# Expert token lists through a table in memory, a split distance that shrinks, and every second down weight left in f32, in a one-core hybrid decoder layer

## The reference

```python
g_sel = argmax(x @ w_rg + b_rg)                    # one of 4 groups per token
top_v, top_i = top_k(e_logits of that group, 2)    # two of its 4 experts
top_w = softmax(top_v) * softmax(g_logits)[g_sel]
gates = sum(one_hot(g_sel * 4 + top_i, 16) * top_w)
for e in range(16):
    h = silu(x @ w_g[e]) * (x @ w_u[e])            # 1024 -> 512
    out += gates[:, e] * (h @ w_d[e])              # 512 -> 1024
```

## Time and profile before

| | |
|---|---|
| median of 3 runs | 964.55 us (960.51 to 964.68) |
| the profiled execution | 964.39 us, span of its trace 962.6 us |
| mean granted clock of TensorE in it | 0.957 of full |
| busy over the span | PE 91%, DVE 68%, ACT 50%, POOL 8% |
| HBM read and written | 170.67 MB and 14.39 MB |

### The profile page before, as it was taken

The page is one execution under the profiler, slowest core; times in us unless marked ns, Lnnn a source line. Parts: engine busy times, 40 slices in busy tenths (PEclk is TensorE's granted clock), DMA queues, the critical chain, the costliest instruction groups (busy, mean ns, idle before and its releaser), DMA issues.

```text
span 962.6 us, 19161 instructions
## 1 busy us (share of the span) xinstructions
PE 876.3 (91%) x8176; PEld 585.2 (61%) x8176; DVE 658.8 (68%) x877; ACT 481.0 (50%) x681; POOL 81.8 (8%) x89
## 2 busy tenths in 40 slices
PE   6999999999999998999999979948899999888683
PEld 4444794856756655444444439947687777776561
DVE  5668769632887766643453344466799999998878
ACT  5434473323554445233223223554597878787842
POOL 8000000003000000000000000000121232111100
PEclk9999999999999999999999999967899999999987
DMA  8711414526731012953432416374899999999852
GB/s 213 168 35 45 125 30 110 155 66 176 188 91 34 25 37 61 372 137 98 121 102 83 122 28 220 127 284 140 305 359 383 399 397 397 381 392 378 331 203 90
DMA packets 122607, 178.20 MB, mean 185 GB/s; under 512 B 13357, under 2 KB 98661, under 8 KB 114326
## 3 DMA queue, kind: packets, MB, share of 16 engines
q1 hardware_dynamic: 116272, 162.76, 49.6%
q0 software_dynamic: 5968, 13.61, 5.2%
q10 hardware_dynamic: 278, 0.56, 0.2%
HBM read 170.67 MB, written 14.39 MB: 192 GB/s over the span
## 4 chain that ended last, share of the span: by engine, by line
PE 64%; DVE 19%; DMA 7%; ACT 6%; issue 3%; DVEq 0%; SPq 0%; ACTq 0%; POOLq 0%
PE bank L980 17%; PE bank L982 17%; PE bank L981 17%; DVE arena L1737 10%; DMA arena<-in_moe_wu 6%; ACT arena L853 3%; PE bank L1193 3%; PE bank L1212 3%; PE bank L1087 1%; PE bank L1202 1%; DVE arena L1844 1%; DMA arena<-x_rows,token_of 1%; DVE arena L1854 1%; ACT arena L935 1%; PE bank L1284 1%
## 5 line engine op out<-in xcount | busy, mean ns | idle before, releaser
L980 PE MATMUL bank<-arena 128*128 128x96 f16 (+3 forms) x2336 | 510.0, 264 | 37.4 <-DVE arena L1844 26.4
L981 PE MATMUL bank<-arena 128*128 128x96 f16 (+3 forms) x2336 | 509.0, 264 | 0.0
L982 PE MATMUL bank<-arena 128*128 128x96 f16 (+3 forms) x2336 | 508.6, 264 | 0.3
L980 PEld LDWEIGHTS bank<-arena 128*128 128x128 f16 (+1 forms) x2336 | 238.2, 102 | 139.4 <-issue 34.1
L982 PEld LDWEIGHTS bank<-arena 128*128 128x128 f16 (+1 forms) x2336 | 237.4, 102 | 77.1 <-issue 1.7
L981 PEld LDWEIGHTS bank<-arena 128*128 128x128 f16 (+1 forms) x2336 | 237.5, 102 | 68.2 <-issue 1.6
L1737 DVE SCALAR_TENSOR_TENSOR arena<-arena 128x2048 f16<-128x2048 f32 x96 | 216.9, 2287 | 49.2 <-ACT arena L853 46.8
L853 ACT ACTIVATE arena<-arena 128x2048 f16<-128x2048 f32 x96 | 180.6, 1904 | 12.5 <-DMA arena<-in_moe_wu 5.5
L620 ACT ACTIVATE arena<-arena 128x1024 f16<-128x1024 f32 (+1 forms) x92 | 92.5, 1007 | 101.3 <-PE bank L982 73.2
L1482 DVE SCALAR_TENSOR_TENSOR arena<-arena 128x1024 f16<-128x1024 f32 (+1 forms) x91 | 103.5, 1163 | 11.7 <-ACT arena L620 10.1
L674 ACT ACTIVATE arena<-bank 128x512 f32<-128x512 f32 x35 | 20.8, 595 | 90.4 <-PE bank L982 90.3
(11 more groups left out here) (275 smaller groups left out, 726.5 us busy)
## 6 DMA issues: line engine op xcount, KB each, us to landing
arena<-in_moe_wg SPq DMA_DIRECT2D x32, 1024.0 KB, 17.4
arena<-in_moe_wu SPq DMA_DIRECT2D x32, 1024.0 KB, 16.1
arena<-in_moe_wd SPq DMA_DIRECT2D x32, 1024.0 KB, 23.6
arena<-in_w_gate SPq DMA_DIRECT2D x32, 512.0 KB, 4.0
arena<-in_w_in SPq DMA_DIRECT2D x31, 512.0 KB, 4.2
arena<-in_w_branch SPq DMA_DIRECT2D x32, 192.0 KB, 3.5
y_rows<-in_c_tab SPq DMA_DIRECT2D x4, 1024.0 KB, 12.5
arena<-in_w_out SPq DMA_DIRECT2D x8, 512.0 KB, 5.3
```

The source lines that it names most:

```text
L980: pe.matmul(outb, lhs[0], rhs[0], start=first, stop=False, skip_group_check=True)
L981: pe.matmul(outb, lhs[0], rhs[1], start=False, stop=False, skip_group_check=True)
L982: return pe.matmul(outb, lhs[1], rhs[0], start=False, stop=last_, skip_group_check=True)
```

## The change

1. **Lists.** The 16-expert one-hots, `all_tokens`, `tell_lists` and `all_slots` go. VectorE computes for each token and choice j the place `rank * 16 + expert` in a table (`spots`, 6 small operations before the lists of the near experts are read). GpSimd stores 8 bytes per token there (token, token + 512 j) with 8 indirect stores of 128 entries, half of them after the gather of expert 0, half after that of expert 1. Then it loads the table (`lists`, 128 x 128 bytes) and stores the weights (1024 single values). Gathers from expert 2 on wait for the table. The weights of the last two experts are fetched by two indirect gathers. The near lists of experts 0 and 1 stay one-hot products. The table is filled with "nowhere" at the kernel's start.
2. **Buffers.** As the large one-hot is gone, chunk 16 takes the twelfth buffer and waits only for the x rows (it took buffer 5, after the split of chunk 5).
3. **Split distance.** ScalarE and VectorE split chunk c + 5 at step c up to step 55, c + 4 from 56 to 63, c + 3 from 64 to 71, and c + 2 from step 72 on.
4. **Down weights in f32.** For odd experts the d chunks aren't split. TensorE multiplies f32 hidden values (`hid_whole`) with the f32 chunk itself: 4 products of 512 columns for a half. Their buffer is free only when TensorE has used it, and SyncE waits for that.
5. **The end.** `add_rows` of the tiles 0 and 1 come at step 92, of tile 2 at step 93, of tile 3 at step 94 (one at each of the steps 92 to 95).

```diff
-LOOK = 5
+LOOK, LOOK_END = 5, 2
+WHOLE = [kind == "d" and e % 2 == 1 for kind, e, _ in STEPS]
+CUT = [c for c in range(len(STEPS)) if not WHOLE[c]]
+SPLITS_AT, _c = {}, FIRST
+for _at in range(len(STEPS)):
+    _upto = _at + (LOOK if _at < len(STEPS) // 2 else max(LOOK_END, LOOK - (_at - len(STEPS) // 2) // 8))
+    SPLITS_AT[_at] = [_i for _i in range(_c, min(_upto + 1, len(STEPS))) if not WHOLE[_i]]
+    _c = max(_c, _upto + 1)
...
-        SLOT = [*range(READY), *range(FIRST), READY, *range(FIRST, READY - 2), READY + 1]
+        SLOT = [*range(READY), *range(FIRST), READY, READY + 1, *range(FIRST, READY - 2)]
...
+        def slot_free(c):
+            last = max((i for i in range(c) if SLOT[i] == SLOT[c]), default=None)
+            if last is None:
+                return None
+            return ("chunk_used", last + 1) if WHOLE[last] else ("split_done", CUT.index(last) + 1)
...
 # GpSimd
+                    if n < 2:
+                        if n == 0:
+                            pool.wait_ge(S("wr_landed"), 96)
+                            pool.wait_ge(S("route_ready"), 2)
+                        for t in range(NT):
+                            pool.indirect_dma_start(out=list_rows, out_offset=bass.IndirectOffsetOnAxis(ap=spots[:, n, t:t + 1], axis=0),
+                                                    in_=entry[:, n, t, :], in_offset=None, bounds_check=P * NE - 1, oob_is_err=False
+                                                    ).then_inc(S("list_stored"), 16)
+                    if n == 1:
+                        pool.wait_ge(S("list_stored"), 16 * 2 * NT)
+                        pool.dma_start(lists[:, :, :].rearrange("p e w -> p (e w)"), list_rows.rearrange("(p e) w -> p (e w)", e=NE)
+                                       ).then_inc(S("list_landed"), 16)
+                        pool.wait_ge(S("route_ready"), 3)
+                        pool.dma_start(weight_rows.rearrange("(j t p) w -> p (j t w)", j=2, p=P), wsel[:, :, :].rearrange("p j t -> p (j t)"),
+                                       allow_slow_non_contiguous=True).then_inc(S("list_stored"), 16)
...
 # ScalarE and VectorE, at the end of step c
-                    if FIRST <= c + LOOK < len(STEPS):
-                        split(c + LOOK)
+                    for i in SPLITS_AT[c]:
+                        split(i)
...
 # TensorE
+                    if WHOLE[c]:
+                        pe.wait_ge(S(f"stage_landed{SLOT[c]}"), landed(c))
+                        v = stage[c].rearrange("p (k n) -> p k n", k=2)
+                        h = hid_whole.rearrange("p (k c) -> p k c", c=CAP)
+                        for k in range(2):
+                            for j in range(2):
+                                last = pe.matmul(y_bank(e)[j][0:CAP, :], h[:, 2 * hf + k, :], v[:, k, 512 * j:512 * (j + 1)],
+                                                 start=hf == 0 and k == 0, stop=hf == 1 and k == 1, skip_group_check=True)
+                        last.then_inc(S("chunk_used"), 1)
+                        continue
...
-                    if c == 3:
-                        all_tokens()
...
 # VectorE
+            link(stt(spot[:, 0, :, :], rank[:, :, :], float(NE), numbers.unsqueeze(1).to_broadcast([P, NT, NE]), ALU.mult, ALU.add))
+            for j in range(2):
+                link(tt(spot[:, 1 + j, :, :], spot[:, 0, :, :], selj[:, j, :, :], ALU.mult))
+                ins = dve.tensor_reduce(rt[:, 13 + j, :, 0:1], spot[:, 1 + j, :, :], axis=AX.X, op=ALU.add)
+                link(ins)
+            sig("route_ready", dve.tensor_copy(spots[:, :, :], rt[:, 13:15, :, 0]))
...
-            for t in range(NT):
-                tell("onehot_ready", tt(*onehot_views(t), ALU.is_equal))
...
-                    if c >= len(STEPS) - NT:
-                        add_rows(c - len(STEPS) + NT)
+                    if c == len(STEPS) - NT:
+                        add_rows(0)
+                        add_rows(1)
+                    elif len(STEPS) - NT < c < len(STEPS) - 1:
+                        add_rows(c - len(STEPS) + NT + 1)
```

More of the change, by code:

```diff
@@ L307, in build @@
         yout = [arena[:, 9216 + D * i:9216 + D * (i + 1)] for i in range(2)]
-        hgT = [[view(19456 + 512 * i + 256 * j, KH * CAP // 2).bitcast(F16) for j in range(2)] for i in range(2)]
+        hgT = [view(19456 + 192 * j, KH * CAP // 2).bitcast(F16) for j in range(2)]
+        hid_whole = view(19456 + 512, KH * CAP)
         yg = [view(STAGE[SLOT[len(STEPS) - NS + t]], 2, D) for t in range(NT)]
@@ new lines, in _ @@
+                    if n == 3:
+                        pool.wait_ge(S("list_stored"), 16 * (2 * NT + 1))
+                        for i in range(LAST):
+                            pool.indirect_dma_start(out=slotw[0:CAP, i:i + 1], out_offset=None, in_=weight_rows,
+                                                    in_offset=bass.IndirectOffsetOnAxis(ap=row_of(ROUTED + i), axis=0),
+                                                    bounds_check=2 * T - 1, oob_is_err=False).then_inc(S("list_landed"), 16)
@@ L1305, in _ @@
             with pe.If(fit):
-                def all_tokens():
-                    pe.wait_ge(S("onehot_ready"), 2 + NT)
-                    for e in range(NE):
-                        for t in range(NT):
-                            last = pe.matmul(ps[4][:, 5 * e:5 * e + 5], onehot[:, t, :].rearrange("p (c e) -> p e c", e=NE)[:, e, :],
-                                             told[:, t, :, e], start=(t == 0), stop=(t == NT - 1))
-                    last.then_inc(S("token_full"), 1)
                 def x_transposes(e):
@@ L1735, in split @@
             def split(c):
-                dve.wait_ge(S("hi_done"), c + 1)
-                tell("split_done", stt(w_lo[c % NW], stage[c], WSCALE, w_hi[c % NW], ALU.mult, ALU.subtract))
+                i = CUT.index(c)
+                dve.wait_ge(S("hi_done"), i + 1)
+                tell("split_done", stt(w_lo[i % NW], stage[c], WSCALE, w_hi[i % NW], ALU.mult, ALU.subtract))
             dve.wait_ge(S("gain2_landed"), 32)
@@ L1741, in _ @@
             link(dve.memset(told[:, :, 1, :], 1.0))
+            link(dve.memset(slotw[:, :], 0.0))
+            for j in range(2):
+                link(dve.tensor_copy(entry[:, j, :, 0].bitcast(U32), tokid))
+                link(ts(entry[:, j, :, 1].bitcast(U32), tokid, float(j * T), None, ALU.add))
             for m in range(KD):
```

163 lines of the change are left out of this document (81 added, 82 removed).

## The result

The changed kernel takes **984.41 us** (median of 4 runs, 980.06 to 989.30); the kernel before, beside it, 963.97 us (4 runs). The ratio is 1.0221, 95% interval [1.0166, 1.0275]: slower by 2.2%; the interval doesn't settle whether by more than 2%. The time lies inside the range of 952 to 986, but above the forecast's own 966 to 982 and 12 us above the 972 predicted. The profiled execution took 980.06 us, the lowest of the four, with a span of 977.8 us: 15.2 us more than the 962.6 of before.

What follows compares the result with a forecast made beforehand. VectorE was taken to pace the stage at first, the weight DMAs at its end, and the distance-2 turn after the change. 872 + 72.1 + 15.9 = 960, plus 10 clock and 1.8 outside the span: 972 us; range 952 to 986, own 966 to 982.

Steps and rivals of the forecast that it cites:

- Part 3, the turn: Last four experts: at distance 2 TensorE waits for ScalarE's and VectorE's splits; 23.1 us an expert with split d.
- With distance 3 ... about 16 us, which hides: Expert stage: with splits three steps ahead, an expert takes about 16 us, under the 18.7 at which chunks land.
- The step that failed: Start of the last four experts' count: chunk 77 split 2 us earlier than 868, so step 77 ends at 872.
- The clock: TensorE in the last four experts: eight waits of 2.8 us or longer, six clock falls at 1.7 us, +10 us.
- chain, end and clock: From step 77 on: 72.1 us to the first last sum, 15.9 from there to the end, 10 for clock falls.
- the signs that the prediction named: Trace from step 72: three TensorE waits of 2.8 us an expert, `x_lo` intervals of 22 us or more, gather before 677.
- Part 4: Odd experts' down chunks whole: VectorE saves 5.0 us, ScalarE 4.3 per odd expert; a TensorE half takes 3.5, +0.9 a step.
- The landings come 0 to 4 us earlier, I take 2: Weight loads: the earlier start of parts 1 and 2 is mostly handed back where chunk 26 waits for step 14.
- loads run dry: Rival: SyncE waits at chunks 26, 38, 50 and so on, DMAs stand at five gates, +3 x 5, 985 us; chance 0.08.
- Parts 1 and 2: Lists and buffer: first gather +1.4 us, table there at 670 to 676, less waiting worth -4 to -6 us from step 8.
- Part 5: End: adds run beside d14 and d15, three tiles to +66.8, the last to +69.4; then 15.9 us from the first last-add.

Runs made afterwards that it cites:

- warm_fill: Changed kernel with 18 products of constants added on TensorE at each second half from step 72 on; 982.13 us, ratio 1.0201 to the kernel before.
- look3: Changed kernel with the split distance shrinking from 5 to 3 and not to 2; 967.20 us, ratio 1.0058 to the kernel before.
- before_shrink3: Kernel before with only a split distance that shrinks from 5 to 3; 961.99 us, ratio 0.9990.
- before_shrink: Kernel before with only the split distance shrinking 5, 4, 3, 2; 980.97 us, ratio 1.0210.
- gate_only: Kernel before, all chunks split, but SyncE reloads buffers of odd experts' down chunks only after TensorE has used them; 966.45 us, ratio 1.0038.
- look5: Changed kernel with the split distance left at 5 throughout; 968.18 us, ratio 1.0045 to the kernel before.
- lists_only: Changed kernel with all down weights split and distance 5, keeping table, earlier buffer and earlier adds; 968.45 us, ratio 1.0061 to the kernel before.
- lists_tail3: Changed kernel with distance shrinking to 3 and whole down weights in experts 13 and 15 alone; 962.31 us, ratio 0.9990 to the kernel before.
- tail3: Kernel before with distance shrinking to 3, d13 and d15 whole, and y-row adds two, one, one at steps 92 to 94; 956.01 us, ratio 0.9941.
- near_first: lists_only with VectorE's operations on the table's places moved behind its near lists; 973.31 us, ratio 1.0091 to the kernel before.
- adds_only: Kernel before with only the y-row adds moved: two tiles at step 92, one at 93, one at 94; 964.59 us, ratio 1.0008.

## Why the prediction was right in sign and 12 us short

The median is 12.4 us above the 972 predicted. The profiled execution, the lowest of the four, is 8.1 above it; what follows accounts for that one.

**Part 3, the turn: right, and most of the matter.** Counted from single durations, the time from the tanh of expert 13 to the first last sum was 72.1 us without the clock; the trace has 961.84 - 886.41 = 75.4, and warm_fill, with its clock at 1.00 in this stretch, 957.92 - 885.86 = 72.1; from tanh to tanh it has 22.9 for the 23.1. "With distance 3 ... about 16 us, which hides" held too (look3, before_shrink3). In the prediction's own steps from the end of step 77, predicted and measured: second u half done and transposed +7.9 and +7.4; d12 +15.9 and +15.4; g14 +23.1 and +24.5; d13 +30.0 and +31.4; g15 +45.7 and +47.9; d14 +60.2 and +64.0; d15 +67.1 and +70.9. In warm_fill d15 comes at +68.6, and the first last sum is still as counted: there the adds of y rows end at +69.5 (counted +69.4), and they hold the end, not TensorE.

**The step that failed is where the chain was hung up.** The text said: "the split of chunk 77 began at 868 as it landed; 2 us earlier, then 4.2 of splits and 1.9 of product, and step 77 ends at 872." It ended at 886.4, 14.4 us later. With a distance of 2 the split of chunk 77 stands in step 75, behind the y output of expert 11, and that waits for TensorE's step 75. The landing of chunk 77 doesn't decide this any more. The rule was in the prediction itself ("only after its own work of step c") and was applied to every step but the first. The nearest row to hang it on is in the trace of before, ScalarE's y output of expert 11:

```profile
878.43 1.06 ACT L935 ACTIVATE arena<-bank 96x512 f32<-96x512 f32 x2
```

From there the prediction's own 7.2 us of y output, two splits and product make 885.6 (measured 886.4, of which the clock has 1.4: warm_fill takes 885.86 - 878.35 = 7.5 for it, the changed kernel 8.9). And 885.6 + 72.1 + 15.9 = 973.6 without the clock, where the text had 960. That this row of before fits so well has luck in it: from the mark to it the kernel before takes 235.0 us, before_shrink 227.9 and the changed kernel 230.9. So the shrinking up to there gains some 7 us that the row doesn't have; the changed kernel's other parts and its mark, 3.3 us later, take most of them back.

**The clock: too large.** Six falls at 1.7 us, +10. In windows of 4 us the changed kernel shows four stretches between 0.57 and 0.67 after 884 us; warm_fill puts their price at 3.6 us in the profiles (957.26 - 877.55 = 79.7 for 954.44 - 878.35 = 76.1, from the y output of expert 11 to the last) and 4.7 to the first last sum. There were fewer falls than six, and fewer long waits than the text's eight of 2.8 us or more: TensorE stood that long four times after 865 us (2.97, 3.25, 3.25 and 3.69 us), and twice more over 2 us. That a part of each fall is hidden as well, since ScalarE and VectorE split on while TensorE is behind, is a guess that no run tests. Put together, step 77 was 14.4 us later than predicted, and from there to the end it took 91.4 us where chain, end and clock had 98.0: 14.4 - 6.6 = 7.8, and the span shows 977.8 - 970 = 7.8. That is a sum made up of differences, not a test of its own; what it says is that a clock term two to three times too large hid nearly half of the wrong starting point.

Of the signs that the prediction named, ScalarE's splits waited for TensorE and not for loads, the low parts of x of experts 13 and 14 were 23.7 us apart (19.2 before), the gather of expert 2 went off at 675.83 and a whole half took 3.5 us. Three waits of 2.8 us an expert didn't come.

**Part 4: durations right, landings wrong.** A whole half takes 3.5 us on TensorE (the two halves of expert 11 have 16 records and 7.03 us), as costed. "The landings come 0 to 4 us earlier, I take 2" failed. Chunk 26 waited for TensorE's step 14, which I put at about 702 us; it went off at 710.4. The first experts ran as early as before or later (the low part of x of expert 2 at 692.7, before 690.2), and TensorE's step 14 is behind that. Chunk 73 was then split as it landed at 863.1, before at 857.5: 5.7 us later. Of all these differences 3.3 us had arisen ahead of the mark, which leaves 2.4 for chunk 73 and 5.0 for chunk 26. The rival "loads run dry" had this mechanism, with five gates; the trace shows the large hole at the first alone, and after 720 us the loads were at 1.02 again. That its 985 us is next to the measured 984.41 is chance. By gate_only it is worth 3.3 us, and since look5 and lists_only are level, the splits that VectorE saves seem to give that back.

**Parts 1 and 2: as counted, but with a price elsewhere.** The eight stores took 1.0 us each with 0.3 between, the table was read back by 675.8 (predicted 670 to 676), the store of 1024 values took 0.96 us (predicted 1), and the first gather was delayed by 1.2 us against the mark (predicted 1.4). The gain came as well: the low parts of x began 5.9 us later than before for expert 0 and at the same time, 708.63, for expert 3. Still the runs with the table and the earlier buffer are 5.0 and 6.3 us above their likes. In profiles, lists_only against before is +0.8 us up to the mark and -0.7 behind it; lists_tail3 against tail3 is +3.2 and +2.5. About 0.3 us more lies outside the span (2.1 for 1.8). So a good part may arise in the mixers, whose code wasn't touched except for the fill of the table, issued at 20.7 us. Of the 7 kernels with the table profiled, 4 show a lower clock between 200 and 235 us (after, look5, lists_tail3 at 0.83; near_first at 0.93), of the 7 without it 1 (before_shrink, 0.83), and these five have the latest marks. That is a hint, no proof: one profile of each. What in the table would set it off, whether the rest of the price is traffic or order, and how much of it is the buffer's stays open.

**Part 5: no gain by itself** (adds_only). In tail3 the low part of the last y is earlier because the splits of d15 are gone from VectorE's queue too; how much of tail3's 6.0 us over before_shrink3 is due to d13 and how much to d15 wasn't tried apart.

In all, from medians: table and buffer +5.0, whole chunks -0.3, distance +16.2. These three lead step by step from the kernel before to the changed one, so that they add up to the whole says nothing; that before_shrink alone has +17.5 does.

## What to carry to other kernels

When a look-ahead is shortened, hang the first step of the hand count on the instruction that now stands before it in the queue, not on the event that released it in the old trace: a turn between engines starts where its slowest member stands. Count the turn at each distance from single durations (2: 23.1 us an expert, 3: 16, loads 18.7), and don't go below the distance whose turn stays under the next bound. Shortening down to it gained nothing by itself (before_shrink3). Leave work out where its engine is full and its successor waits, here d13 and d15, and not in every second expert, where buffers are held longer (lists_tail3 against look3).

## What the runs showed of the hardware that was not expected

- The clock of TensorE can come out differently in the same code: between 225 and 235 us it was 1.00 or 0.83 from one kernel's profile to another's, and the mixers' end ranged from 643.0 to 649.2 us. A single pair of profiles can be 3 us apart before the changed code starts; a mark at the end of the unchanged part takes that out.
- Idle stretches of TensorE of up to 3.7 us, six of them over 2 us in the last four experts, came with four stretches of low clock, which cost 3.6 to 4.7 us in all (one profile of each kernel). One fall seen in the trace before, multiplied by six, had promised 10.
- An indirect store of 128 entries of 8 bytes held GpSimd for 0.98 to 1.06 us, and the last of eight had landed 3.5 us after its issue ended; one of the eight took 2.06.
